# Window attention of the third mixer: probabilities turned by a scaled identity, outputs computed turned

## Chip, cores and metric

The kernel is one launch on one core of one Trainium2 chip. The metric is device time in microseconds (us). TensorE (PE) multiplies, VectorE (DVE) and ScalarE (ACT) work on tiles of 128 partitions, GpSimd (POOL) does small element-wise work, SyncE (SP) issues DMAs. Each engine runs its own instructions in program order, and engines wait for each other through counting semaphores.

## The reference, cut to what matters

The reference is two stacked blocks of a sequence model (256 tokens, width 1024, float32): mixers of several kinds, cross attention, dense and expert feed-forward layers. The change touches one part, the attention half of the third mixer. It has 8 query heads of width 64, 2 key/value heads, a causal window of 128 keys, and a "sink" logit for each head that enters the denominator alone:

```python
def sliding_window_attention(q, k, v, sinks):
    ...
    s = jnp.einsum('bnqhgd,bnkhd->bnhgqk', qb, kb) * (ATT_HEAD_DIM ** -0.5)
    s = jnp.where(valid[None, :, None, None], s, -1e30)
    m = jnp.maximum(jnp.max(s, axis=-1, keepdims=True), sink)
    p = jnp.exp(s - m)
    denom = jnp.sum(p, axis=-1, keepdims=True) + jnp.exp(sink - m)
    o = jnp.einsum('bnhgqk,bnkhd->bnqhgd', p / denom, vb)

def even_mixer_2(...):
    ...
    y_att = sliding_window_attention(q, k, v, sinks)
    y = jnp.concatenate([y_lru.astype(h.dtype), y_att.astype(h.dtype)], axis=-1)
    return y @ w_out
```

## The kernel before

The program is a list of stages: `mix0`, `cross0`, `ffn0`, `mamba`, `cross1`, `ffn1`, `mix2`, `ffn2`, `gdn`, `moe`. The third mixer is `mix2`, the function `lru_and_window`. The 256 tokens are two tiles of 128 partitions (TT = 2, P = 128). The stage projects the queries (`take_queries`, L4018 to L4037), normalises and rotates them on DVE, projects the gate (L2005 of the profile), and calls `paired_attention` (L939). Its result and that of the recurrence (`gated_scan`) are the two halves of `yT`, the turned input of the output projection (`project`, L565 of the profile); its `take` adds to `h` and opens the next stage's front.

`paired_attention` works on four pairs of heads. In step n it emits, in this order: `turn_queries(n)`, `scores(n-1)` with `weigh` for both heads, `turn_weights(n-2)` for both heads, `values(n-3)` for both heads, and then `during[n]`, a piece of the recurrence on DVE (`inputs` in step 1, `gated_scan` in step 2). Each engine runs its share of these in exactly this order; nothing is reordered.

- `turn_queries` (L989): two transposes on PE, one copy on ACT (L998).
- `scores` (L1011): for each token tile and each head one 64-row matmul of 256 columns; the two heads of a pair lie on the two halves of the rows.
- `weigh`: on DVE scale and mask (L1028), row maximum (L1031), maximum with the sink (L1033), negation (L1035); on ACT the exponentials with their row sums (L1044) and that of the sink (L1046).
- `turn_weights`: on DVE sum plus sink (L1057) and the reciprocal (L1059). On PE three transposes of 128x128 (L1069): three of the four blocks of a head, since the future block is empty. PE waits for the bank and for `weights[i]`, ACT's mark, and not for the reciprocal. ACT copies the turned blocks to SBUF (L1079, L1080).
- `values` (L1095): three matmuls a head with the turned probabilities as weights and the 64 value columns moving. DVE (L1105) multiplies the result by the reciprocals while it moves it from PSUM to `y`, tokens on partitions.

After the last head `transpose_tiles` turns `y` with eight transposes on PE (L379) and two copies on ACT (L387) into `yT`. Then `project` starts.

`unseen(engine, marks)` gives the waits an engine still needs. A mark is a lane and a count, one lane for each engine, and a count covers all that the engine issued before it. PSUM banks are taken in turn from eight (`take_bank`).

Of the kernel before, what the change touches and what calls it, by code (L numbers as in the profile page):

```python
# [18 lines left out]
ALU = mybir.AluOpType  # L19
# [3 lines left out]
P = 128  # L23
T = 256
TT = T // P
D = 1024
KD = D // P
# [134 lines left out]
def build(nc, a, out, stages=None):  # L162
    with ExitStack() as ctx:  # L163
# [53 lines left out]
        ident = const("ident")  # L217
# [3 lines left out]
        def take_bank():  # L221
            turn[0] += 1
            return banks[(turn[0] - 1) % BANKS]
# [15 lines left out]
        def room(cols, dt=F32):  # L239
            ap = arena[:, top[0]:top[0] + cols]  # L240
            top[0] += cols
            assert top[0] <= ARENA, top[0]
            return ap if dt == F32 else ap.bitcast(dt)
# [16 lines left out]
        def room3(n, m):  # L260
            return room(n * m).rearrange("p (n m) -> p n m", m=m)

        V, S, M, G = (Lane(new_semaphore, n) for n in ("vector", "scalar", "tensor", "gpsimd"))
# [3 lines left out]
        def unseen(eng, *marks):  # L267

            for m in marks:
                if isinstance(m, list):  # L270
                    yield from unseen(eng, *m)
                elif m is not None and m[1] > waited.get((eng.engine, m[0].name), 0):
                    waited[eng.engine, m[0].name] = m[1]
                    yield m
# [90 lines left out]
        def transpose_tiles(src, n_k, ready, dst, gain=None, gain_ready=None):  # L365

            marks = []
            for k0 in range(0, n_k, 2):
                ks = range(k0, min(k0 + 2, n_k))
                bank = take_bank()  # L370

                @block.tensor
                def _(pe):
                    for due in unseen(pe, bank.free, ready(k0) if callable(ready) else ready):
                        pe.wait_ge(*due)
                    for k in ks:
                        for t in range(TT):
                            at = (k - k0) * T + t * P
                            last = pe.transpose(bank.ap[:, at:at + P], src[:, t, k * P:(k + 1) * P], ident)  # L379
                    last.then_inc(*M.tick())  # L380
                turned = M.at()

                if gain is None:
                    @block.scalar
                    def _(act):
                        act.wait_ge(*turned)
                        act.copy(dst[:, k0:k0 + len(ks), :],  # L387
                                 bank.ap[:, 0:len(ks) * T].rearrange("p (k t) -> p k t", t=T)).then_inc(*S.tick())
                    bank.free = S.at()
                else:  # L390
                    @block.vector
                    def _(dve):
                        for due in unseen(dve, gain_ready):
                            dve.wait_ge(*due)
                        dve.wait_ge(*turned)
                        for k in ks:
                            dve.tensor_scalar(dst[:, k, :], bank.ap[:, (k - k0) * T:(k - k0 + 1) * T],
                                              gain[:, k:k + 1], None, ALU.mult).then_inc(*V.tick())
                    bank.free = V.at()
            return V.at() if gain is not None else S.at()  # L400
# [535 lines left out]
                        step(n - back)  # L936
            return V.at()

        def paired_attention(qkv, H, KVH, N, scale, y, ready, mask, sink, during):  # L939


            HK = H + KVH
            heads = [{n: room(TT) for n in ("m", "nm", "sum", "es")} for _ in range(H)]
            bufs = [{n: room(512) for n in ("s", "p", "pt")} for _ in range(4)]
            qT, kT = [room(T) for _ in range(2)], room3(KVH, T)
            twice = room(TT * KVH * P).rearrange("p (t j n) -> p t j n", t=TT, j=KVH)
            half = [slice(g * N, g * N + N) for g in range(2)]
            copied, weights, inverse, turned_p = {}, {}, {}, {}
            q_used, p_used, pt_used = {}, {}, {}
            value = lambda t, i: qkv[:, t, (HK + i * KVH // H) * N:(HK + i * KVH // H + 1) * N]  # L950
# [98 lines left out]
            def turn_weights(i):  # L1049
                b, sm = bufs[i % 4], heads[i]  # L1050
                bank = take_bank()

                @block.vector
                def _(dve):
                    for due in unseen(dve, weights[i]):
                        dve.wait_ge(*due)
                    dve.tensor_tensor(sm["sum"], sm["sum"], sm["es"], ALU.add).then_inc(*V.tick())  # L1057
                    dve.wait_ge(*V.at())
                    dve.reciprocal(sm["sum"], sm["sum"]).then_inc(*V.tick())  # L1059
                inverse[i] = V.at()  # L1060

                @block.tensor
                def _(pe):
                    for due in unseen(pe, bank.free, weights[i]):
                        pe.wait_ge(*due)
                    for kt in range(TT):
                        for t in range(kt, TT):
                            at = kt * T + t * P
                            last = pe.transpose(bank.ap[:, at:at + P], b["p"][:, t * T + kt * P:t * T + (kt + 1) * P],  # L1069
                                                ident)  # L1070
                    last.then_inc(*M.tick())
                turned = p_used[i] = M.at()

                @block.scalar
                def _(act):
                    for due in unseen(act, pt_used.get(i - 4)):
                        act.wait_ge(*due)
                    act.wait_ge(*turned)
                    act.copy(b["pt"][:, 0:T], bank.ap[:, 0:T]).then_inc(*S.tick())  # L1079
                    act.copy(b["pt"][:, T + P:2 * T], bank.ap[:, T + P:2 * T]).then_inc(*S.tick())  # L1080
                bank.free = S.at()
                turned_p[i] = S.at()

            def values(i):
                b, sm = bufs[i % 4], heads[i]
                bank = take_bank()

                @block.tensor
                def _(pe):
                    for due in unseen(pe, bank.free, turned_p[i]):  # L1090
                        pe.wait_ge(*due)
                    for t in range(TT):
                        for kt in range(t + 1):
                            at = kt * T + t * P
                            last = pe.matmul(bank.ap[:, t * N:(t + 1) * N], b["pt"][:, at:at + P], value(kt, i),  # L1095
                                             start=(kt == 0), stop=(kt == t))
                    last.then_inc(*M.tick())
                have = pt_used[i] = M.at()

                @block.vector  # L1100
                def _(dve):
                    for due in unseen(dve, inverse[i]):
                        dve.wait_ge(*due)
                    dve.wait_ge(*have)
                    dve.tensor_tensor(y(i), bank.ap[:, 0:TT * N].rearrange("p (t n) -> p t n", t=TT),  # L1105
                                      sm["sum"].unsqueeze(2).to_broadcast([P, TT, N]), ALU.mult).then_inc(*V.tick())
                bank.free = V.at()

            turn_keys()
# [2744 lines left out]
        def lru_and_window():  # L3854
            LW, H, KVH, N = 512, 8, 2, 64
            NT4 = LW // P
# [14 lines left out]
            yT = room3(KD, T)  # L3871
# [1 line left out]
            x = room3(NT4, T)  # L3873
            gate = room3(NT4, T)
            qkv = room3(TT, (H + 2 * KVH) * N)
            y = room3(TT, H * N)
            keep = top[0]
            normed = norm_turned(h, D, None, xT, g_in, params_landed, lambda: None)

# [28 lines left out]
            for i in range(NT4):  # L3908
                bank = take_bank()
# [8 lines left out]
                have = M.at()  # L3918
# [122 lines left out]
            rotated = query_scaled(1, sums)  # L4041

            def take(i, ps, mark):
                @block.scalar
                def _(act):
# [2 lines left out]
                return S.at()  # L4048
            project_turned(a["e_w_in_2"][0], LW, NT4, normed, take)
            gate_ready = S.at()  # L4050
            have = paired_attention(qkv, H, KVH, N, N ** -0.5, lambda i: y[:, :, i * N:(i + 1) * N], rotated,
                                    const("band"), sinks, [lambda: None, inputs, gated_scan])
            lru_ready = made["lru"]
            turned = transpose_tiles(y, 4, have, yT[:, NT4:KD, :])
            pass_over_first_slot(2)
            top[0] = front_top
            front = fronts["ffn2"] = ffn_front("ffn2", ("ln_ffn_2", 0), dense_src)
            turn[0] += (4 - turn[0]) % BANKS
            project(yT, KD, a["e_w_out_2"][0], D, [turned, lru_ready],
                    front["take_between"]([turned, lru_ready, V.at(), M.at(), G.at()]))  # L4060


        def deltanet():
# [606 lines left out]
        last = [lane.at() for lane in (V, S, M, G) if lane.count]  # L4670
# [26 lines left out]
```

## Time and profile before

| | us |
|---|---|
| three runs | 2626.55, 2632.03, 2633.16 |
| median of the runs | 2632.03 |
| the profiled execution's own time | 2627.18 |
| its span, first to last instruction | 2625.3 |
| PE busy | 2448.7 (93% of the span) |
| DVE busy | 1805.2 (69%) |
| ACT busy | 1424.6 (54%) |
| mean granted TensorE clock | 0.958 of full speed |

The attention around the change runs from about 1136.5 to 1171.5 us of the span. A float32 matmul appears in the trace as two records on PE, a transpose as one. The start of a row is in us from the span's start; the time of a merged row (x12) is from the first start to the last end.

### The profile page before, as it was taken

What the parts mean: (1) busy time and instruction counts of PE and PEld (TensorE: products, weight loads), DVE (VectorE), ACT (ScalarE), POOL (GpSimd) and SP (SyncE); (2) the same over time, 40 slices, a digit from 0 to 9 for tenths busy, and PEclk for the clock granted to TensorE, in tenths of its full rate; (3) what the DMA queues carried; (4) which work ended last, traced back from release to release, by engine and by line L of the source; (5) the groups of instructions that cost most, each with busy time, mean ns of one, the idle gap of its engine ahead of it and who ended that gap; (6) DMA issues with size and microseconds to landing.
All of it is one profiled execution on the core that took longest, in us unless ns stands there. A gap on an engine that the chain in (4) does not pass through costs nothing. (4 is left out here: it accounts for less than half of the span.)

```text
span 2625.3 us, 39490 instructions
## 1 busy us (share of the span) xinstructions
PE 2448.7 (93%) x14932; PEld 2054.5 (78%) x14932; DVE 1805.2 (69%) x2444; ACT 1424.6 (54%) x1900; POOL 322.7 (12%) x215
## 2 busy tenths in 40 slices
PE   7889889988998999989998996899999999999998
PEld 6457569988885799767997986788888888888887
DVE  3665654567565555573555764889988988889986
ACT  4242244345552444333445541677778787777776
POOL 4110200014442000000003431000000000000000
PEclk9889999999899999979998998899999999999999
DMA  7510325544231454414545402899999999999995
GB/s 256 174 38 29 128 96 192 187 145 138 94 129 64 140 177 165 163 65 141 178 164 175 161 2 81 325 375 379 377 386 364 393 369 386 381 378 377 375 382 214
DMA packets 180009, 573.83 MB, mean 219 GB/s; under 512 B 11966, under 2 KB 81726, under 8 KB 136764
## 3 DMA queue, kind: packets, MB, share of 16 engines
q1 hardware_dynamic: 175932, 558.27, 57.2%
q0 software_dynamic: 2992, 11.01, 1.6%
q10 hardware_dynamic: 976, 3.03, 0.3%
q8 instruction: 76, 1.25, 0.2%
q14 instruction: 33, 0.27, 0.0%
HBM read 564.16 MB, written 6.29 MB: 217 GB/s over the span
## 5 line engine op out<-in xcount | busy, mean ns | idle before, releaser
L3481 DVE TENSOR_TENSOR moe_weights_low<-ring,moe_weights_high 128x1024 fp32r<-128x1024 f32 x672 | 779.8, 1217 | 95.5 <-ACT moe_weights_high L3730 95.5
L3730 ACT CAST moe_weights_high<-ring 128x1024 fp32r<-128x1024 f32 x672 | 687.0, 1053 | 108.8 <-PE banks L258 106.0
L256 PE MATMUL banks<-moe_weights_high,moe_rows_high 128*128 128x512 f32 x896 | 355.4, 397 | 3.1 <-DVE moe_rows_low L3486 2.5
L258 PE MATMUL banks<-moe_weights_low,moe_rows_high 128*128 128x512 f32 x896 | 350.6, 391 | 0.0
L257 PE MATMUL banks<-moe_weights_high,moe_rows_low 128*128 128x512 f32 x896 | 350.0, 391 | 0.0
L256 PE MATMUL banks<-ffn_x_high,ffn_weights_high 128*128 128x256 f32 x1056 | 299.1, 283 | 0.7 <-DVE ffn_x_low L3104 0.7
L257 PE MATMUL banks<-ffn_x_high,ring_low 128*128 128x256 f32 x1056 | 297.5, 282 | 0.0
L258 PE MATMUL banks<-ffn_x_low,ffn_weights_high 128*128 128x256 f32 x1056 | 297.4, 282 | 0.0
L3280 DVE TENSOR_TENSOR ring_low<-ring,ffn_weights_high 128x2048 fp32r<-128x2048 f32 x60 | 134.8, 2289 | 130.2 <-ACT ffn_weights_high L3254 130.2
L256 PEld LDWEIGHTS banks<-ffn_x_high,ffn_weights_high 128*128 128x128 f32 x1056 | 199.1, 188 | 4.4 <-DVE ffn_x_low L3104 1.3
L257 PEld LDWEIGHTS banks<-ffn_x_high,ring_low 128*128 128x128 f32 x1056 | 199.4, 189 | 2.6
L258 PEld LDWEIGHTS banks<-ffn_x_low,ffn_weights_high 128*128 128x128 f32 x1056 | 199.9, 189 | 0.0
L256 PEld LDWEIGHTS banks<-moe_weights_high,moe_rows_high 128*128 128x128 f32 x896 | 169.0, 189 | 37.1 <-DVE moe_rows_low L3486 2.7
L258 PEld LDWEIGHTS banks<-moe_weights_low,moe_rows_high 128*128 128x128 f32 x896 | 168.9, 188 | 36.5
L257 PEld LDWEIGHTS banks<-moe_weights_high,moe_rows_low 128*128 128x128 f32 x896 | 169.2, 189 | 34.0
L3254 ACT CAST ffn_weights_high<-ring 128x2048 fp32r<-128x2048 f32 x60 | 111.3, 1902 | 136.4 <-DMA ring<-in_ffn_w 76.1
L456 POOL TENSOR_TENSOR arena<-arena,consts 128x2 f32<-128x2 f32 (+3 forms) x47 | 51.5, 1096 | 1074.1 <-DVE arena L502 760.3
L256 PE MATMUL banks<-moe_weights_high,moe_hidden_high 128*128 128x512 f32 x448 | 176.9, 395 | 0.0
L258 PE MATMUL banks<-moe_weights_low,moe_hidden_high 128*128 128x512 f32 x448 | 174.7, 390 | 0.0
L257 PE MATMUL banks<-moe_weights_high,moe_hidden_low 128*128 128x512 f32 x448 | 174.4, 389 | 0.0
L600 POOL TENSOR_TENSOR ring_low<-ring,pieces_high 128x1024 fp32r<-128x1024 f32 (+2 forms) x63 | 157.0, 2496 | 115.4 <-ACT pieces_high L586 115.3
L256 PE MATMUL banks<-x_high,pieces_high 128*128 128x256 f32 (+2 forms) x528 | 158.1, 299 | 5.9 <-DVE x_low L445 5.6
(630 smaller groups left out, 4662.1 us busy)
## 6 DMA issues: line engine op xcount, KB each, us to landing
ring<-in_moe_gate_pieces SPq DMA_DIRECT2D x112, 1024.0 KB, 6.9
ring<-in_moe_up_pieces SPq DMA_DIRECT2D x112, 1024.0 KB, 7.2
ring<-in_moe_down_pieces SPq DMA_DIRECT2D x112, 1024.0 KB, 7.1
ring<-in_ffn_w SPq DMA_DIRECT2D x66, 1024.0 KB, 7.8
ring<-in_od_w_in SPq DMA_DIRECT2D x10, 2048.0 KB, 8.1
ring<-in_o_w_in SPq DMA_DIRECT2D x8, 2048.0 KB, 8.8
ring<-in_e_ffn_w_gate SPq DMA_DIRECT2D x11, 1024.0 KB, 5.5
ring<-in_e_ffn_w_up SPq DMA_DIRECT2D x11, 1024.0 KB, 8.1
```

The costliest lines, as they stand in the source:

```text
L256: pe.matmul(out_, lh, rh, start=start, stop=False)
L257: pe.matmul(out_, ll, rh, start=False, stop=False)
L258: return pe.matmul(out_, lh, rl, start=False, stop=stop)
L456: pool.tensor_tensor(x, x, const("minus_half")[:, 0:n], ALU.pow).then_inc(*G.tick())
L600: pool.tensor_tensor(low_view, view, high.bitcast(F32), ALU.subtract).then_inc(*G.tick())
L3254: act.copy(high[b][:, c], units[b][:, c]).then_inc(up_high, 1)
L3280: dve.tensor_tensor(low[b][:, c], units[b][:, c], high[b][:, c].bitcast(F32), ALU.subtract).then_inc(up_low, 1)
L3481: dve.tensor_tensor(lo[:, b], piece, hi[:, b].bitcast(F32), ALU.subtract).then_inc(sems["lo_done"], 1)
L3730: act.copy(hi[:, b * 1024:(b + 1) * 1024], piece).then_inc(sems["hi_done"], 1)
```

## The change

Three things are altered in `paired_attention`, and its caller. First, DVE builds for each head a tile of `roots`: two 128x128 diagonal matrices, the identity times the reciprocal row sums of the two token tiles; PE turns the probabilities by a plain matmul with it as the moving operand in place of a transpose, and waits for the mark `inverse[i]` that stands behind it. Second, `values` takes the value columns as weights and moves the turned probabilities, so that the output has the head's 64 columns on partitions and tokens along the row; the two heads of a pair write the two halves of the partitions of one shared bank. Third, one plain DVE copy for each pair moves that bank to `yT`; the buffer `y`, the multiplication by the reciprocals and the call of `transpose_tiles` are gone.

```diff
@@ -936,12 +936,14 @@
                         step(n - back)
             return V.at()
 
-        def paired_attention(qkv, H, KVH, N, scale, y, ready, mask, sink, during):
+        def paired_attention(qkv, H, KVH, N, scale, yT, ready, mask, sink, during):
 
 
             HK = H + KVH
             heads = [{n: room(TT) for n in ("m", "nm", "sum", "es")} for _ in range(H)]
             bufs = [{n: room(512) for n in ("s", "p", "pt")} for _ in range(4)]
+            roots = [room3(TT, P) for _ in range(4)]
+            shared = {}
             qT, kT = [room(T) for _ in range(2)], room3(KVH, T)
             twice = room(TT * KVH * P).rearrange("p (t j n) -> p t j n", t=TT, j=KVH)
             half = [slice(g * N, g * N + N) for g in range(2)]
@@ -1057,17 +1059,22 @@
                     dve.tensor_tensor(sm["sum"], sm["sum"], sm["es"], ALU.add).then_inc(*V.tick())
                     dve.wait_ge(*V.at())
                     dve.reciprocal(sm["sum"], sm["sum"]).then_inc(*V.tick())
+                    for due in unseen(dve, p_used.get(i - 4)):
+                        dve.wait_ge(*due)
+                    dve.wait_ge(*V.at())
+                    dve.tensor_tensor(roots[i % 4], ident.unsqueeze(1).to_broadcast([P, TT, P]),
+                                      sm["sum"].unsqueeze(2).to_broadcast([P, TT, P]), ALU.mult).then_inc(*V.tick())
                 inverse[i] = V.at()
 
                 @block.tensor
                 def _(pe):
-                    for due in unseen(pe, bank.free, weights[i]):
+                    for due in unseen(pe, bank.free, weights[i], inverse[i]):
                         pe.wait_ge(*due)
                     for kt in range(TT):
                         for t in range(kt, TT):
                             at = kt * T + t * P
-                            last = pe.transpose(bank.ap[:, at:at + P], b["p"][:, t * T + kt * P:t * T + (kt + 1) * P],
-                                                ident)
+                            last = pe.matmul(bank.ap[:, at:at + P], b["p"][:, t * T + kt * P:t * T + (kt + 1) * P],
+                                             roots[i % 4][:, t, :], start=True, stop=True)
                     last.then_inc(*M.tick())
                 turned = p_used[i] = M.at()
 
@@ -1082,8 +1089,10 @@
                 turned_p[i] = S.at()
 
             def values(i):
-                b, sm = bufs[i % 4], heads[i]
-                bank = take_bank()
+                b, g = bufs[i % 4], i % 2
+                if g == 0:
+                    shared["bank"] = take_bank()
+                bank = shared["bank"]
 
                 @block.tensor
                 def _(pe):
@@ -1092,18 +1101,17 @@
                     for t in range(TT):
                         for kt in range(t + 1):
                             at = kt * T + t * P
-                            last = pe.matmul(bank.ap[:, t * N:(t + 1) * N], b["pt"][:, at:at + P], value(kt, i),
+                            last = pe.matmul(bank.ap[half[g], t * P:(t + 1) * P], value(kt, i), b["pt"][:, at:at + P],
                                              start=(kt == 0), stop=(kt == t))
                     last.then_inc(*M.tick())
                 have = pt_used[i] = M.at()
-
-                @block.vector
-                def _(dve):
-                    for due in unseen(dve, inverse[i]):
-                        dve.wait_ge(*due)
+                if g == 0:
+                    return
+
+                @block.vector
+                def _(dve):
                     dve.wait_ge(*have)
-                    dve.tensor_tensor(y(i), bank.ap[:, 0:TT * N].rearrange("p (t n) -> p t n", t=TT),
-                                      sm["sum"].unsqueeze(2).to_broadcast([P, TT, N]), ALU.mult).then_inc(*V.tick())
+                    dve.tensor_copy(yT[:, i // 2, :], bank.ap[:, 0:T]).then_inc(*V.tick())
                 bank.free = V.at()
 
             turn_keys()
@@ -3873,7 +3881,6 @@
             x = room3(NT4, T)
             gate = room3(NT4, T)
             qkv = room3(TT, (H + 2 * KVH) * N)
-            y = room3(TT, H * N)
             keep = top[0]
             normed = norm_turned(h, D, None, xT, g_in, params_landed, lambda: None)
 
@@ -4048,16 +4055,15 @@
                 return S.at()
             project_turned(a["e_w_in_2"][0], LW, NT4, normed, take)
             gate_ready = S.at()
-            have = paired_attention(qkv, H, KVH, N, N ** -0.5, lambda i: y[:, :, i * N:(i + 1) * N], rotated,
+            have = paired_attention(qkv, H, KVH, N, N ** -0.5, yT[:, NT4:KD, :], rotated,
                                     const("band"), sinks, [lambda: None, inputs, gated_scan])
             lru_ready = made["lru"]
-            turned = transpose_tiles(y, 4, have, yT[:, NT4:KD, :])
             pass_over_first_slot(2)
             top[0] = front_top
             front = fronts["ffn2"] = ffn_front("ffn2", ("ln_ffn_2", 0), dense_src)
             turn[0] += (4 - turn[0]) % BANKS
-            project(yT, KD, a["e_w_out_2"][0], D, [turned, lru_ready],
-                    front["take_between"]([turned, lru_ready, V.at(), M.at(), G.at()]))
+            project(yT, KD, a["e_w_out_2"][0], D, [have, lru_ready],
+                    front["take_between"]([have, lru_ready, V.at(), M.at(), G.at()]))
 
 
         def deltanet():
```

## Rows read from the trace of the kernel before

**Rows 1.** The page's first part: busy time of each engine over the span.

```profile
PE 2448.7 (93%) x14932; PEld 2054.5 (78%) x14932; DVE 1805.2 (69%) x2444; ACT 1424.6 (54%) x1900; POOL 322.7 (12%) x215
```

**Rows 2.** Engines by stretch: length, then PE, PEld, DVE, ACT, POOL busy, PEclk, DMA.

```profile
1137.00:1138.00 1.00, 0.63 (x6) 0.39 (x4) 0.00 (x0) 0.77 (x3) 0.00 (x0) 0.90 0.00 0
1138.00:1171.00 33.00, 27.81 (x116) 21.61 (x116) 22.18 (x62) 16.58 (x63) 0.00 (x0) 0.50 0.00 1
1175.00:1176.00 1.00, 1.00 (x3) 0.51 (x2) 1.00 (x2) 0.19 (x1) 0.00 (x0) 0.82 0.00 0
```

**Rows 3.** Groups by line and form, 1134 to 1172 us: busy, mean ns | idle before.

```profile
L1095 PE MATMUL banks<-arena 128*128 128x64 f32 x48 | 10.5, 414 | 0.0
L1011 PE MATMUL banks<-arena 64*128 64x256 f32 x32 | 8.3, 670 | 0.6 <-ACT arena L998 0.6
L1069 PE MATMUL banks<-consts,arena 128*128 128x128 f32 x24 | 7.1, 433 | 4.2 <-ACT arena L1046 4.2
```

**Rows 4.** Timeline of the attention's first half: start, us, engine, line [idle before <-releaser].

```profile
1129.62 2.97 PE L2005 MATMUL banks<-xT,ring 128*128 128x256 f32 x13
...
1140.86 2.08 PE L1011 MATMUL banks<-arena 64*128 64x256 f32 x8
1143.61 0.90 PE L1069 MATMUL banks<-consts,arena 128*128 128x128 f32 x3 [0.67 <-ACT arena L1046]
1146.09 0.63 PE L989 MATMUL banks<-consts,arena 128*128 128x128 f32 x2
1146.37 0.67 DVE L1028 SCALAR_TENSOR_TENSOR arena<-banks,consts 128x512 f32<-128x512 f32 x1
1146.65 2.08 PE L1011 MATMUL banks<-arena 64*128 64x256 f32 x8
1149.91 0.15 DVE L1057 TENSOR_TENSOR arena<-arena 128x2 f32<-128x2 f32 x1
1150.10 0.17 DVE L1059 RECIPROCAL arena<-arena 128x2 f32<-128x2 f32 x1
1150.44 1.25 DVE L4015 TENSOR_TENSOR_SCAN arena<-arena 128x256 f32<-128x256 f32 x2
1152.13 2.66 PE L1095 MATMUL banks<-arena 128*128 128x64 f32 x12
1152.87 0.68 DVE L1028 SCALAR_TENSOR_TENSOR arena<-banks,consts 128x512 f32<-128x512 f32 x1
1154.72 2.08 PE L1011 MATMUL banks<-arena 64*128 64x256 f32 x8
```

**Rows 5.** The same timeline at the attention's end.

```profile
1163.13 5.22 PE L1095 MATMUL banks<-arena 128*128 128x64 f32 x24
1168.89 1.94 PE L379 MATMUL banks<-consts,arena 128*128 128x128 f32 x8 [0.54 <-DVE arena L1105]
1171.51 22.76 PE L565 MATMUL banks<-ring,arena 128*128 128x512 f32 x48 [0.68 <-ACT arena L387]
```

**Rows 6.** Timeline elsewhere: rotation of the queries, and the first cross attention.

```profile
1133.27 0.43 DVE L782 TENSOR_TENSOR arena<-arena,consts 128x256 f32<-128x256 f32 x1
1133.61 0.42 DVE L783 TENSOR_TENSOR arena<-arena,consts 128x256 f32<-128x256 f32 x1
337.20 1.16 PE L2810 MATMUL banks<-arena 128*128 128x128 f32 x8 [1.01 <-DVE arena L2795]
338.41 1.03 PE L2764 MATMUL banks<-arena 128*128 128x256 f32 x4
342.33 0.42 DVE L2840 COPY arena<-banks 128x256 f32<-128x256 f32 x1
```

**Rows 7.** Start of the third mixer: transposes in PE's timeline, then engines by stretch.

```profile
1076.13 3.50 PE L379 MATMUL banks<-consts,arena 128*128 128x128 f32 x16 [4.94 <-DVE arena L517]
...
1076.00:1079.00 3.00, 2.87 (x14) 2.87 (x15) 2.76 (x8) 0.00 (x0) 0.00 (x0) 0.56 0.54 106
1079.00:1080.00 1.00, 0.64 (x3) 0.23 (x2) 1.00 (x3) 0.00 (x0) 0.00 (x0) 0.61 0.78 224
```

## The prediction

> **What bounds the kernel now.** I read the page's first part, then the stretch around the attention by windows, the groups by line in it, and the timeline. Over the span PE is the busy engine [rows 1]. In the attention it is busy for 27.8 of 33 us, more than DVE (22.2) or ACT (16.6), but at a granted clock of 0.50, that is 1.2 GHz [rows 2]. The clock fell at about 1137.8 (0.90 in the slice 1137 to 1138), after PE's last matmuls before the attention had ended at 1132.59 [rows 4], and came back at about 1175.36 (0.82 in the slice from 1175), 3.85 us after the output projection began at 1171.51 [rows 2, 5].
>
> The PE groups are the 48 records of the values, the 32 of the scores and the 24 transposes of the probabilities; the latter wait 4.2 us in all, for ACT [rows 3]. The order in the timeline matters most. The first head's probabilities are turned from 1143.61. DVE reaches that head's sum (L1057) only at 1149.91, since ahead of it in its queue stands the weighing of the next pair, two heads from 1146.37 to 1149.91, 3.54 us [rows 4]. Today that lag costs nothing: only the multiplication after the values reads the reciprocal.
>
> **The change part by part.** The sum is made against the profiled execution (2627.18, of which the span is 2625.3), from the last instant at which nothing differs.
>
> *The new wait.* PE now turns pair n-2 only when DVE has passed its `roots`, and a lane's count covers what is ahead: the weighing of pair n-1, which in turn waits for the scores of pair n-1, emitted on PE just before. So PE stands between its scores and its turning for a whole weighing, and behind the waiting turn are queued the values, the next pair's scores and so DVE's next weighing. From the end of the scores to PE's go: hand-over 0.05, two heads 3.54, sum to reciprocal 0.19 [rows 4], reciprocal to dependent 0.20 (its 0.17 plus a hand-over), the 128x256 product 0.43 L782 of [rows 6], hand-over 0.05: 4.46 us. The second head's product follows 0.74 later (0.19 + 0.20 + a start-to-start of 0.34 [rows 6]) while PE turns the first, and so is hidden; with a faster PE it costs at most 0.1 a pair. Price of the product itself: between 0.34 and twice 0.34 (if it ran like two separate 128x256 passes); I take 0.43, the nearest row.
>
> *Turning.* Three transposes a head become three plain float32 matmuls, two records each: the second cross attention's form shows eight records for four such matmuls L2810 of [rows 6]. At 1.2 GHz a record of this size takes 0.216 from start to start: twelve records of the values fill 1152.13 to 1154.72, and eight transposes of 128 columns take 1.94 less a last one of 0.42 [rows 4, 5]. A pair is 12 x 0.216 = 2.59 in place of 1.30. At 2.4 GHz L2810 gives (1.16 - 0.28)/7 = 0.124 a record, 1.5 a pair. Bounds: 0.107 (half of 0.216) and 0.216.
>
> *Values.* Twelve records a pair stay, 64 columns moving become 128 and the weights 64 columns wide. A record of 128 columns costs 0.216 as well, so nothing changes cold; hot it is 0.124. Bounds for a pair: 1.30, if the two heads' halves ran side by side as the two row halves of the scores do (eight records of 256 columns in 2.08 [rows 4]), though here all six records of one head come before the other's; and 2.59 plus a fill of 0.2 at each change. I take 2.59.
>
> The Trainium skill (TensorEngine Tiling, Key Properties) says that changing the tiling mode drains TensorE. That speaks against outputs of 64 partitions between full-width matmuls, and by it each of some eight changes would cost up to the 0.2 by which a record outlasts the start-to-start, 1.6 in all. The trace does not show it for row halves: the values, full width, start at 1152.13 and the 64-row scores 2.59 later, twelve times the 0.217 that the transposes of [rows 5] take from start to start ((1.94 - 0.42)/7). I put it at nothing.
>
> *The end.* The last values now lead to a copy of 128x256 on DVE, 0.42 L2840 of [rows 6] plus two hand-overs: 0.52. Before, from the last values' end (1168.35) to the projection it was 3.16 [rows 5]; eight transposes and two ACT copies go. The other three copies stand in DVE's queue; that of pair 1 holds up the roots of pair 3. Eight multiplications of 0.29 go from DVE, eight products of 0.43 come. ACT loses two copies, its other work lies under PE's and DVE's. Banks: values and final transposes take one four times in place of ten, and by the order each comes round long after it was drained. DMA: none is added or moved, and none runs here (share 0.00 [rows 2]).
>
> *The chain.* Pair 0: DVE at its sum at 1149.91, where it is today; go at 1149.91 + 0.87 = 1150.78 (today the turning was done by then). Turning to 1153.37, queries 0.56 (1146.09 to 1146.65), scores 2.08: 1156.01 at 1.2 GHz. `gated_scan`, 2.43 on DVE (1150.44 to 1152.87), lies beside it.
>
> Now the clock. With the projection as the measure it comes back 3.85 us into dense work, so at 1154.63, and the remaining 1.38 is halved: scores end at 1155.3. Go for pair 1: 1159.8. PE has stood 4.5 us; the clock fell 5.2 us after the last dense matmul in [rows 2, 4], so it is about to fall, and I let the next burst start at 1.2 GHz.
> - Turning 1, values 0, scores 3: 2.59 + 2.59 + 2.08 = 7.26, the first 3.85 slow and 3.41 halved: ends 1165.3; go for pair 2 at 1169.8.
> - Turning 2, values 1: 5.38 with the fill; 3.85 + 0.77: ends 1174.4. Copy started (0.05 + 0.34) and the last two heads' roots (0.87): go at 1175.7. A pause of 1.3 us, clock kept.
> - Turning 3, values 2 and 3: 36 records at 0.124 and a fill of 0.15: 4.6, ends 1180.3. Copy: projection at 1180.8.
>
> That is 9.3 us later than 1171.51. The projection then starts at full clock, and the 3.85 us that it ran slow are halved: -1.9. Sum +7.4: 2634.6 for the profiled execution. That one lies at the low end of the runs; I put the sum on the mean of the three (2630.6), which gives 2638.0; on the median, 2639.4.
>
> A rule on the clock. The Trainium skill (TensorE: Matmul & The Clock Gate, Part 4) says that transposes don't count as PE-busy and don't bring the clock back; by it, plain matmuls in their place would be what brings it back here, and otherwise bursts with transposes would run slow. The trace shows otherwise: sixteen transposes alone, from 1076.13 after an idle 4.9 us, and the clock went from 0.5 up at about 1079.8 [rows 7]. So I credit the new matmuls with their larger share of streaming, not with their kind.
>
> **Rivals.**
> *The clock stays at 1.2 GHz.* For it: it did for 37 us here, with PE 84% busy. Against: these were 64-row scores, and values whose 64 moving columns fill half of each record. Price: scores 1156.0; go 1160.5; 7.26 to 1167.7; go 1172.2; to 1177.6; go 1178.8; 36 x 0.216 + 0.2 to 1186.8; projection 1187.3. Plus 15.8, with a slow start of the projection as now: 2646.4.
>
> *The clock comes back once and holds through the pauses.* Then from 1155.3: go 1159.8; 24 x 0.124 + 1.03 (half of the scores' 2.08) = 4.0; go 1168.3; 3.1, 1.26; 4.6; 0.5: projection 1177.8, +6.3 - 1.9 = +4.4: 2635.0. Against: pauses of 4.5 us, near the 5.2 in which it fell.
>
> *Faster: the wait doesn't bind.* If DVE had the roots ready when PE comes to turn (each pair's go at or before the end of the scores, where the chain above has it 4.46 behind), the attention would keep its pace: dense from 1151.46 with the clock back at 1155.3, DVE through the last sums at about 1162.5, roots and one turning 1.3, 24 records of values at 0.124 with fill 3.2, copy 0.5: projection 1167.5, -4.0 - 1.9 = -5.9: 2624.7. It decides from a lag below 2 us a pair in place of 4.46: the lags of pairs 0 to 2 stand on the chain in full, and three of 2 us take back the 5.9. Against it stands DVE's program order.
>
> **How the numbers follow.** Forecast 0.55, clock stays slow 0.22, clock holds 0.13, no binding wait 0.10. About 0.3% (7.9 us) is what the measurement can tell from no change. The forecast's own range is +5 to +10, a bit less than half of it above 7.9: 0.25 slower, 0.30 same. The slow clock gives 0.22 slower; the holding clock 0.13 same; the last case 0.06 same and 0.04 faster. Together faster 0.04, same 0.49, slower 0.47. Range: from the holding clock on the low runs (2626.6 + 4.4) to the slow clock with a little more (2647).
>
> **What would show it.** PE's idle time before L1069 (now the plain matmuls) put down to DVE's roots, about 4.4 us in each of the second and third pairs and 7.8 in the first; 48 records of turning in place of 24; the projection starting 6 to 10 us later than 1171.5 and at clock 1.0; no L379 in the stretch; clock above 0.5 within the attention. It is wrong if these waits are short, if the clock is 0.5 throughout (then near 2646), or if the new 64-column values take other than 0.216 or 0.124 a record.

## Result and profile after

| | before | after |
|---|---|---|
| median of eight runs each, us | 2631.0 | 2639.77 |
| lowest to highest | 2626.55 to 2634.83 | 2636.24 to 2645.07 |
| profiled execution, own time | 2627.18 | 2639.53 |
| its span | 2625.3 | 2637.6 |
| ratio after to before, 95% interval | | 1.0038 [1.0027, 1.0049] |

The kernel became slower by 0.38%, 10.0 us on 2631.0, with an interval of 7.1 to 12.9; the ratio is taken over all the runs, and the two medians lie 8.8 apart. The forecast was 2638.0, +7.4.

A whole execution is a poor ruler for this change: the same program's runs are spread over 8 us. Aligning the starts of the same PE records in the two profiled executions shows where: the one of after is 1.7 us late at 1120 us, before anything differs, 9.3 late at 1221, and 12.3 from about 1600 to the end. So 7.6 us arise around the attention and 4.7 before and behind it, in stages that the change does not touch. For each kernel I therefore also give the *stage length*: from the start of the first record of the scores to the start of the last record of the output projection. Before it is 63.2 us, after 70.4: **+7.2**.

The stretches of the attention in the profile after (columns as in [rows 2]), the first over all of it, the others where the clock changes:

```profile
1140.00:1183.00 43.00, 23.81 (x134) 19.12 (x134) 25.48 (x66) 17.29 (x62) 0.00 (x0) 0.65 0.00 1
...
1156.00:1158.00 2.00, 1.62 (x10) 0.89 (x8) 0.34 (x2) 0.80 (x3) 0.00 (x0) 0.81 0.00 0
...
1160.00:1162.00 2.00, 0.00 (x0) 0.00 (x0) 1.83 (x8) 1.50 (x8) 0.00 (x0) 0.54 0.00 0
...
1166.00:1168.00 2.00, 2.00 (x17) 1.38 (x13) 0.42 (x1) 0.00 (x0) 0.00 (x0) 0.75 0.00 0
...
1170.00:1172.00 2.00, 0.00 (x0) 0.00 (x0) 1.86 (x7) 1.36 (x6) 0.00 (x0) 0.60 0.00 0
...
1176.00:1178.00 2.00, 1.50 (x12) 1.21 (x10) 0.47 (x2) 0.29 (x2) 0.00 (x0) 0.69 0.00 0
```

Of 43 us PE is busy 23.8, where it was 27.8 of 33 [rows 2], and the mean clock is 0.65 in place of 0.50: PE's clock has risen and PE stands still more. What it waits for, by groups of the same stretch (columns as in [rows 3]):

```profile
L1076 PE MATMUL banks<-arena 128*128 128x128 f32 x48 | 10.3, 396 | 18.5 <-DVE arena L1059 18.5
L1013 PE MATMUL banks<-arena 64*128 64x256 f32 x32 | 6.7, 550 | 0.2 <-ACT arena L1000 0.2
L1104 PE MATMUL banks<-arena 128*64 128x128 f32 x48 | 5.7, 350 | 0.0
```

The 4.2 us that the transposes waited for ACT [rows 3] have become 18.5 us for DVE. The releaser named is the sum L1059, an inferred event of DVE's chain. PE starts 0.15 us after the end of the pair's first roots L1065 (for the first pair 1152.86 and 1153.01), so it is the roots that PE waits for. The timeline shows the order:

```profile
1140.36 2.08 PE L1013 MATMUL banks<-arena 64*128 64x256 f32 x8 [0.19 <-ACT arena L1000]
...
1152.05 0.15 DVE L1059 TENSOR_TENSOR arena<-arena 128x2 f32<-128x2 f32 x1
1152.23 0.17 DVE L1061 RECIPROCAL arena<-arena 128x2 f32<-128x2 f32 x1
1152.43 0.43 DVE L1065 TENSOR_TENSOR arena<-consts,arena 128x256 f32<-128x256 f32 x1
...
1153.01 2.90 PE L1076 MATMUL banks<-arena 128*128 128x128 f32 x12 [7.94 <-DVE arena L1059]
...
1156.26 1.36 PE L1013 MATMUL banks<-arena 64*128 64x256 f32 x8
...
1157.70 0.69 DVE L1030 SCALAR_TENSOR_TENSOR arena<-banks,consts 128x512 f32<-128x512 f32 x1 [1.66 <-PE banks L1013]
...
1162.23 2.90 PE L1076 MATMUL banks<-arena 128*128 128x128 f32 x12 [4.61 <-DVE arena L1059]
...
1165.06 2.03 PE L1104 MATMUL banks<-arena 128*64 128x128 f32 x12
...
1167.02 1.13 PE L1013 MATMUL banks<-arena 64*128 64x256 f32 x8
...
1172.76 2.90 PE L1076 MATMUL banks<-arena 128*128 128x128 f32 x12 [4.60 <-DVE arena L1059]
...
1178.83 1.64 PE L1076 MATMUL banks<-arena 128*128 128x128 f32 x12 [1.34 <-DVE arena L1059]
...
1180.40 1.81 PE L1104 MATMUL banks<-arena 128*64 128x128 f32 x24
...
1182.72 11.86 PE L565 MATMUL banks<-ring,arena 128*128 128x512 f32 x27 [0.52 <-DVE arena L1114]
```

PE and DVE now take turns. While DVE weighs and builds roots, PE stands; while PE turns, multiplies the values and scores, DVE has at most the second head's roots, a piece of the recurrence and a copy to do. The four waits are 7.94, 4.61, 4.60 and 1.34 us.

### The profile page after: what moved, and what is told of

Read it like the earlier page. It is cut to its first block and busy times, and to the rows that moved or that the text cites. A ratio compares the mean times of both kernels' runs of the same rounds, so it can differ in the third digit from the quotient of the medians.

```text
span 2637.6 us, 39515 instructions
## 1 busy us (share of the span) xinstructions
PE 2448.9 (93%) x14948; PEld 2055.6 (78%) x14948; DVE 1809.0 (69%) x2448; ACT 1424.5 (54%) x1898; POOL 322.8 (12%) x215
## 5 line engine op out<-in xcount | busy, mean ns | idle before, releaser
L3489 DVE TENSOR_TENSOR moe_weights_low<-ring,moe_weights_high 128x1024 fp32r<-128x1024 f32 x672 | 780.4, 1221 | 95.3 <-ACT moe_weights_high L3738 95.2
```

The source lines that it names most:

```text
L3489: dve.tensor_tensor(lo[:, b], piece, hi[:, b].bitcast(F32), ALU.subtract).then_inc(sems["lo_done"], 1)
```

## Experiments

Lengths are stage lengths, and intervals are those of the ratio to the kernel before, which was run again beside them (medians 2629.8 to 2631.3).

The clock can differ between two executions of the same work. A later kernel of this section (outputs by pair) runs exactly as the kernel before until 19.7 us after the first scores: each of PE's first 66 records starts within 0.03 us of its fellow. Then its clock came back, and that of the kernel before did not. First both kernels up to that moment, then both behind it, the kernel before ahead of the other each time (columns as in [rows 2]):

```profile
1138.00:1158.00 20.00, 16.04 (x64) 10.77 (x64) 16.81 (x41) 10.88 (x41) 0.00 (x0) 0.50 0.00 0
1142.00:1162.00 20.00, 16.02 (x63) 10.73 (x63) 16.57 (x41) 10.88 (x41) 0.00 (x0) 0.51 0.00 0
...
1158.00:1167.00 9.00, 8.48 (x40) 8.11 (x41) 4.79 (x20) 4.99 (x22) 0.00 (x0) 0.50 0.01 2
1162.00:1171.00 9.00, 6.87 (x53) 5.93 (x53) 5.62 (x22) 6.24 (x26) 0.00 (x0) 0.96 0.01 2
```

So one profiled execution gives one stage length, and it holds the luck of where the clock changed. That goes for the 63.2 us of the kernel before too. For nine of the eleven kernels (the changed one and these ten) the ratio gives a larger difference to the kernel before than the stage lengths do, by 2.0 us in the mean of all eleven; so in the profiled execution of the kernel before the stage was perhaps some 2 us longer than it mostly is (an estimate). A difference of 1 to 3 us between two lengths decides nothing by itself.

| kernel | median, us | ratio to before | length |
|---|---|---|---|
| roots first | 2629.74 | 1.0003 [0.9988, 1.0017] | 62.3 |
| wait alone | 2641.89 | 1.0046 [1.003, 1.0062] | 75.8 |
| plain matmuls, no wait | 2629.26 | 0.9993 [0.9982, 1.0004] | 57.2 |
| transposes, no wait | 2629.04 | 0.999 [0.9975, 1.0004] | 58.5 |
| filled pauses | 2634.91 | 1.0015 [1.0001, 1.0029] | 69.4 |
| one half | 2645.54 | 1.0056 [1.0035, 1.0076] | 74.2 |
| roots on POOL | 2630.86 | 1.0 [0.9988, 1.0012] | 62.1 |
| roots first, products on POOL | 2631.22 | 1.0001 [0.9988, 1.0014] | 60.5 |
| outputs by pair | 2628.08 | 0.9995 [0.9984, 1.0005] | 57.1 |
| outputs by pair, products on POOL | 2626.93 | 0.9994 [0.9983, 1.0005] | 59.7 |

**The wait by itself.** The kernel before, with one mark added to PE's wait:

```diff
-                    for due in unseen(pe, bank.free, weights[i]):
+                    for due in unseen(pe, bank.free, weights[i], inverse[i]):
```

> The kernel before with nothing but the new wait: PE waits for the reciprocal's mark before its transposes. No product, no plain matmul, no turned values. Theory of the wait: the chain per pair is scores, weighing 3.54, sum and reciprocal 0.41, transposes 1.3, values 2.6, all at 1.2 GHz since these records do not bring the clock back; the projection starts about 11 us later than before, time about 2642, so the wait alone costs more than the whole change and the change's other parts give a few us back. Rival (records): within 3 us of the kernel before, 2631.

Measured: ratio 1.0046, stage length 75.8, +12.6; the projection starts 11.5 us later after the first scores (44.8 in place of 33.3). PE in its timeline:

```profile
1154.23 1.51 PE L1069 MATMUL banks<-consts,arena 128*128 128x128 f32 x6 [7.47 <-DVE arena L1057]
...
1162.31 1.51 PE L1069 MATMUL banks<-consts,arena 128*128 128x128 f32 x6 [4.14 <-DVE arena L1057]
...
1172.43 1.51 PE L1069 MATMUL banks<-consts,arena 128*128 128x128 f32 x6 [4.14 <-DVE arena L1057]
...
1177.20 1.51 PE L1069 MATMUL banks<-consts,arena 128*128 128x128 f32 x6 [0.81 <-DVE arena L1057]
```

The waits are those of the changed kernel less the product (0.47 to 0.53 us each), and the clock is 0.50 from the first scores to the projection. So by the stage lengths the wait costs more than the whole change, and the change's other parts, with the clock that came back during them, gave 5.4 us of it back. By the ratios the wait alone is 2 us dearer, which their intervals don't tell apart. The rival of the doubled records falls.

**The place in DVE's queue.** All instructions of the changed kernel, with the roots emitted before the next weighing (`build_roots` holds the three DVE instructions that stood in `turn_weights`):

```diff
                     turn_queries(n)
+                if 0 <= n - 2 < pairs:
+                    for g in range(2):
+                        build_roots(2 * (n - 2) + g)
                 if 0 <= n - 1 < pairs:
                     scores(n - 1)
```

> The changed kernel with one thing moved: in each step DVE's sum, reciprocal and roots of pair n-2 are emitted ahead of the weighing of pair n-1 instead of behind it. Every instruction stays. Theory (the cost of the change is PE's wait for a place in DVE's queue behind the next pair's weighing): PE's waits before the turning fall from 7.9, 4.6, 4.6 and 1.3 us to under 2.5 each, the projection starts near the place it has in the kernel before (some 10 us earlier than in the changed kernel, measured from the first weighing), time about 2629, 8 to 10 us below the changed kernel. Rival (the doubled records of the turning and the added DVE products are the cost): these are all still there, so the time stays within 3 us of the changed kernel's 2639.8.

Measured: 8.1 us shorter than the changed kernel, and the median 10.0 lower, at that of the kernel before. The four waits became 4.4, 2.7, 0.3 and 2.6, not all under 2.5 as expected: the first pair's roots stand behind `inputs`, the second's behind `gated_scan`, and those of the last two wait for the exponentials that DVE's own weighing releases. One wait of each kind:

```profile
1143.47 2.90 PE L1079 MATMUL banks<-arena 128*128 128x128 f32 x12 [4.37 <-DVE arena L1058]
...
1156.49 1.81 PE L1079 MATMUL banks<-arena 128*128 128x128 f32 x12 [0.27 <-ACT arena L1048]
```

**No wait.** The plain matmuls move the constant identity, and the kernel leaves out the division by the sums:

```diff
-                    for due in unseen(pe, bank.free, weights[i], inverse[i]):
+                    for due in unseen(pe, bank.free, weights[i]):
...
-                                             roots[i % 4][:, t, :], start=True, stop=True)
+                                             ident, start=True, stop=True)
```

> The changed kernel without the need for the wait: the plain matmuls move the constant identity instead of the roots, so PE waits only for the exponentials; DVE still builds the roots, the outputs come out turned, and the division by the sums is left out of the result. Theory of the wait: the double records and the products are cheap, the projection starts 4 to 7 us earlier than in the kernel before and at full clock, time about 2625 (5 to 8 below the kernel before). Rival (records): slower than the kernel before by 2 to 6 us, since 24 plain matmuls and 8 products are still added.

Measured: stage length 57.2, 6.0 less than before and 13.2 less than the changed kernel. The projection starts 4.1 us earlier after the first scores, at full clock, as expected. The whole time doesn't follow: 0.9993, with an interval of -4.7 to +1.1 us, where 5 to 8 us less were expected. Its profiled execution was 8.0 us late before the attention, 1.9 behind it and 8.6 at the end, which shows the spread from untouched stages. PE now waits for the exponentials, 4.7 us, and twice, 1.9, for what the trace puts down to DVE:

```profile
PE banks L1076 <- ACT arena L1048: 4.7, 5, 1.5
PE banks L1076 <- DVE arena L1065: 1.9, 2, 0.9
```

**What the second record costs.** The same with transposes in place of the plain matmuls:

> The changed kernel with the turning by transposes as before, waiting for the exponentials only; DVE still makes the unused roots, the values come out turned, and the division by the sums is left out. It differs from the kernel with the plain matmuls and no wait (57.2 us from the first scores to the last projection record) only in 24 records less on PE. Theory (the doubled records lie beside DVE's chain): 56 to 58.5. Rival (they stand on the path): 52 to 54, that is 24 records of 0.216 less at 1.2 GHz, or 2.6 less at 2.4 GHz.

Measured: 58.5, no shorter but 1.3 longer. Twenty-four records less bought nothing: in both kernels the last values start 26.8 us after the first scores, and the 1.3 us arise behind that. The values took 3.19 here, mostly at 1.2 GHz, and 1.81 there at 2.4. The last values and the stretches, of this kernel and then of the one with plain matmuls:

```profile
1168.85 3.19 PE L1104 MATMUL banks<-arena 128*64 128x128 f32 x24
...
1142.00:1173.00 31.00, 23.80 (x109) 16.03 (x110) 25.10 (x66) 16.17 (x61) 0.00 (x0) 0.52 0.00 1
```

```profile
1173.01 1.81 PE L1104 MATMUL banks<-arena 128*64 128x128 f32 x24
...
1146.00:1176.00 30.00, 22.59 (x134) 17.00 (x135) 25.09 (x66) 16.50 (x62) 0.00 (x0) 0.77 0.00 1
```

With more records PE was busy less, since the clock was 0.77 and not 0.52. DVE is busy for 25.1 us in both, of 31 and of 30. That the last values start at the same place at two different clocks of PE fits a pace set by DVE's chain; no run here changes that chain alone at one clock.

**The clock in the pauses.** Four matmuls of 256 columns ahead of each pair's turning:

```diff
-                    for due in unseen(pe, bank.free, weights[i], inverse[i]):
+                    for due in unseen(pe, bank.free):
+                        pe.wait_ge(*due)
+                    if i % 2 == 0:
+                        for _ in range(4):
+                            pe.matmul(bank.ap[:, 0:T], ident, kT[:, 0, :], start=True, stop=True)
+                    for due in unseen(pe, weights[i], inverse[i]):
                         pe.wait_ge(*due)
```

> The changed kernel with four extra matmuls of 256 columns on PE in each pause before a pair's turning, their result overwritten: 1.7 us of PE at 2.4 GHz, 3.4 at 1.2 GHz, less than the pause of 4.6. Theory (part of what the pauses cost is the clock, which falls in each of them): the granted clock stays at full speed from the second pair on, the projection starts 2 to 4 us earlier than in the changed kernel, time about 2637. Rival (the clock in the attention does not matter, only DVE's chain does): no earlier than the changed kernel, 2640, or later by what of the extra work sticks out.

Measured: 69.4, only 1.0 less than the changed kernel. The extra work did not hold the clock: it fell in the first pause, and 1.2 and 1.5 us after PE had taken up its work behind the second and third. So the expectation failed, in the clock and in its price. The turnings of the four pairs start 12.6, 21.7, 31.6 and 37.7 us after the first scores, against 12.6, 21.9, 32.4 and 38.5 in the changed kernel; ahead of the last one the extra work stuck out, and no wait remained there. The lower median (2634.9) goes beyond what the stage shows, and I draw nothing from it. What a clock held at full speed would give stays open.

**Two heads side by side.** Both heads of a pair on the lower 64 partitions, and two copies:

```diff
-                            last = pe.matmul(bank.ap[half[g], t * P:(t + 1) * P], value(kt, i), b["pt"][:, at:at + P],
+                            last = pe.matmul(bank.ap[half[0], g * T + t * P:g * T + (t + 1) * P], value(kt, i), b["pt"][:, at:at + P],
...
-                    dve.tensor_copy(yT[:, i // 2, :], bank.ap[:, 0:T]).then_inc(*V.tick())
+                    for j in range(2):
+                        dve.tensor_copy(yT[half[j], i // 2, :], bank.ap[half[0], j * T:(j + 1) * T]).then_inc(*V.tick())
```

> The changed kernel with both heads of a pair written to the lower 64 partitions of the shared bank (side by side in columns) and moved to their places by two DVE copies in place of one, so that the records of the two heads can't run on two column halves of the array at once. From the first scores to the last record of the projection the changed kernel takes 70.4 us. Theory (the values are cheaper than forecast because the two heads' records run side by side): here each pair's twelve records stand 0.21 apart at 1.2 GHz and 0.11 at 2.4 GHz with no overlap, 0.5 us more for each of the first two pairs and 1.0 more for the last two together, 0.3 to 0.7 more for copies; 72.5 to 73. Rival (64 weight columns are simply faster to run): the starts stay 0.06 and 0.05 apart in places, and the length stays within 0.8 of 70.4.

Measured: 74.2, 3.8 more, beyond the expected 2.1 to 2.6. The records now start 0.21 or 0.11 apart, a few further, and none under 0.108; in the changed kernel many follow another by 0.05 or 0.06. The last turning starts 0.7 us later here, and from it to the projection it is 7.0 us in place of 3.9. That holds the missing overlap, the second copy, and the clock, which was at 1.2 GHz for 3.4 us of it; the projection itself ran at 2.4 GHz, as in the changed kernel. That the starts stand apart is shown, then; what the missing overlap costs in time isn't separated from the clock.

```profile
1170.37 2.39 PE L1104 MATMUL banks<-arena 128*64 128x128 f32 x12
...
1187.13 3.86 PE L1104 MATMUL banks<-arena 128*64 128x128 f32 x24
```

**Roots on POOL.** The four operations on the idle engine:

> The changed kernel with the sum, the reciprocal (power -0.5, squared) and the roots made on POOL, which is idle here, so that PE's wait no longer stands behind DVE's weighing; four dependent POOL operations a head. Theory of the wait: PE can turn some 3 us after the head's exponentials, and DVE is relieved of 1.1 us a head; the length from the first scores to the last projection record is 58 to 62 against 70.4 of the changed kernel and 63.2 of the kernel before; time 2626 to 2630. Rival (POOL is too slow: over 2.5 us a head, so that its chain takes DVE's place as the bound): 63 to 68.

Measured: 62.1, between the two, at the edge of the theory's range, and 8.3 less than the changed kernel; the median is 2630.9. On POOL a head takes 2.0 us (0.79 for the product, 0.70 for the power, 0.28 and 0.24), and PE waits 8.2 us for it in place of 18.5 for DVE: the wait got shorter, not free.

**Looking for a better kernel.** With the roots first, two products of 128x1024 moved from DVE to POOL:

> The kernel with the roots ahead of the next weighing, and besides two products of the recurrence (128x1024 each, 1.2 us on DVE) moved to POOL, to take work off the DVE chain that now sets the pace. The length from the first scores to the last projection record was 62.3 with the roots first. Theory (DVE's queue is what sets it): 1 to 2.5 us less, 60 to 61.3, time about 2628. Rival (the exponentials' hand-over sets it, DVE only waits longer for them): 62 or more.

Measured: 60.5, 1.8 less, inside the theory's range. But with the work off DVE the first pair's turning starts 1.3 us earlier and the last pair's only 0.5 (27.1 in place of 27.6); the other 1.3 of the length arise behind it, where the clock came back 3.3 us sooner. So 0.5 us is what DVE's queue can be credited with, and the whole time resolves nothing. Then the kernel before with each pair's outputs turned inside the loop (two transposes and one ACT copy a pair), alone and with the same two products moved:

> The kernel before with one thing moved: the outputs are turned pair by pair inside the loop, two transposes and one ACT copy each as soon as DVE has written the pair, in place of eight transposes and two copies after the last head. No wait on the reciprocals, no plain matmuls. Theory (the only part of the change that saves time on the path besides the clock is the tail of 3.16 us): the tail is halved, two pairs' transposes of 0.43 come into PE's chain near the end; length from the first scores to the last projection record 61.5 to 62.5 against 63.2. Rival (the tail is not on the path or PE pays it back in full): 63 or more.

> The same, and the two products of the recurrence (128x1024) moved from DVE to POOL. Theory (before the change too DVE's queue sets the pace of the attention, with PE at 1.2 GHz close behind): 1 to 2.4 us less than with the outputs by pair alone, length 59.5 to 61, time about 2628. Rival (PE at 1.2 GHz sets the pace): within 0.5 of the kernel with the outputs by pair alone.

Measured: 57.1 and 59.7. The first is far below its expected 61.5 to 62.5 because its clock came back 20.2 us after the first scores, in the middle of the loop, and held; in the second it came back after 19.5 and fell once more. The last values of the second start 1.65 us earlier, 23.0 in place of 24.65, and then take 5.7 us in place of 3.0. So the order of these two lengths is the clock's doing, and neither pair of rivals is decided by the lengths. What the moved turning did is seen at the end: from the last values to the projection it is 1.4 us in place of 3.16, at 2.4 GHz. Their times, 0.9995 and 0.9994, can't be told from the kernel before. None of the versions that compute everything beats it by more than the measurement resolves; but the changed kernel's 2639.8 lies 8 to 13 us above all five (roots first, POOL, by pair).

## Why the prediction was right

The stage in the profile after runs 2.14 us late where the change begins to act: DVE's first sum starts at 1152.05 and not 1149.91 [rows 4]. With that taken off:

| step | forecast | measured |
|---|---|---|
| go, pair 0 | 1150.78 | 1150.87 |
| go, pair 1 | 1159.8 | 1160.1 |
| go, pair 2 | 1169.8 | 1170.6 |
| go, pair 3 | 1175.7 | 1176.7 |
| last values end | 1180.3 | 1180.1 |
| projection starts | 1180.8 | 1180.6 |
| projection faster by | 1.9 | 1.9 |
| sum | +7.4 | +7.2 |

*The wait* was right in place, cause and price: 4.61 and 4.60 us where the sum had 4.46, with a hand-over from the roots to PE of 0.15 and not 0.05. The experiment with the wait alone measured 11.5 where that arithmetic at 1.2 GHz gave about 11, and moving the roots ahead of the weighing, with every instruction kept, took the cost away.

*Turning* was right but for its edges. At 1.2 GHz a record follows another after 0.213, not 0.216, but the first step is 0.34 and the one to the values 0.35: 2.83 from the first record to the values where I had 2.59. At 2.4 GHz most steps are 0.111, and with two longer ones the mean is 0.124, as forecast (the division as it stands, 0.88 by 7, gives 0.126).

*Values* were mis-sized. I took 2.59 a pair at 1.2 GHz and 3.0 for the last two together. Measured 2.03, about midway to the lower bound of 1.30, and 1.81, where that bound, halved by the clock, is 1.30 for both pairs. I had set the bound aside because one head's records come before the other's. In the trace the second head's first record starts at 1165.55, beside the first head's, which run to 1166.18; with both heads on one half (the "one half" kernel) no start follows another by less than 0.108.

*The clock* came back 3.8, 4.8 and 4.5 us after the starts of the bursts, not 3.85 each, and fell 2.6 and 2.3 us after PE's last work. The 5.2 of the forecast left out PE's transposes: in the kernel before the clock fell 1.2 us after these had begun at 1136.56, behind an idle time of 4.0. The forecast's step (lost in each long pause, kept in the short one) held; the later returns cost about what the values gave back. That is luck, and so is part of the agreement of the two sums: in the kernel before the clock stayed at 1.2 GHz up to the projection, where the same work in another execution saw it back after 20.2 us. Against such an execution the change's stage length would have come out larger than +7.2.

*The change of tiling mode* costs something, and I had put it at nothing. The last start of the turning and the first of the values lie 0.35 us apart in the kernel after, where the same step between full-width matmuls in the kernel before has 0.21. The step from the values to the scores, which I had read as free, has 0.35 in both; the twelve records' 2.59 hid it, since the first step among the 64-column values is only 0.11. So a change costs 0.14 us at 1.2 GHz (and 0.09 at 2.4, 0.205 in place of 0.111), and the three new ones some 0.4 in all. The Trainium skill (TensorEngine Tiling, Key Properties) says that changing the tiling mode drains TensorE, and the trace agrees. The term was small.

*Transposes and the clock.* I had read from [rows 7] that transposes bring the clock back. Of the twelve profiled executions it did come back right behind those sixteen transposes in seven, 3.6 to 3.8 us after their start; in these it had fallen only 0.2 to 0.4 us after that start. In the other five it had fallen 1.4 to 1.7 us before them, and came back 8.6 to 8.8 us after their start, 4 us into the matmuls that follow. In the attention the two kernels without the wait differ (clock 0.52 with transposes, 0.77 with plain matmuls), but in the kernel with outputs by pair, where all turning is by transposes, it came back in the loop and was 0.96 behind that. The Trainium skill (TensorE: Matmul & The Clock Gate, Part 4) says that transposes don't count as PE-busy in the same way and that the full clock doesn't engage for them; the seven executions speak against that. No run here separates the kind of record from the rest of the stage. What brought the clock back in the changed kernel, the forecast's larger share of streaming or something else, stays open.

*The rest.* The measured ratio says 10.0 us with 7.1 to 12.9, and the stage accounts for 7.2, at the lower edge. The remainder isn't resolved; in the profiled executions of the ten experiments the untouched stages behind the attention added between -3.2 and +6.8 us. The chances (0.47 slower by over 0.3%, 0.49 within it) split on a sum of 7.4 next to a bound of 7.9. The measured 10.0 lies beyond the bound, on the side that had the slightly smaller chance.

## What to carry to other kernels

Before an engine is made to wait for a mark, look at what stands ahead of that mark in the producer's queue: a cheap producer (here 0.8 us of DVE work) behind an expensive neighbour is as late as the neighbour, and if the neighbour needs the waiting engine's last result, two overlapping engines become one chain. Moving the producer ahead of its neighbour gave back 8.1 us of the stage and 10.0 of the medians with every instruction kept. Moves of a few us inside one stage are better seen in that stage's length in the trace than in the whole time, where the same program differs by more. But a length of one execution holds the clock's luck, so look where in the stage the difference arises, and what the clock was there.

## What was not expected of the hardware

- Matmuls with 64 output partitions for two heads overlapped on the two column halves though all of one head's records come first in the program: at 2.4 GHz starts 0.05 to 0.06 us apart against 0.11 with both on one half.
- Twice the records for the turning did not lengthen the stage: with and without them the last values start 26.8 us after the first scores.
- The same 66 records of PE, with starts equal within 0.03 us, were followed by a return of the clock to 2.4 GHz in one execution (outputs by pair, 20.2 us after the first scores) and by 1.2 GHz up to the projection in another (the kernel before, 37 us).
